# First tile's picks in two halves, its first expert rows gathered from the first half on

## The reference

```python
def ada_mod(c, w, b):
    return jnp.einsum('bd,de->be', jax.nn.silu(c), w) + b

def peer_ffn(h, w_q, sub_keys, peer_u, peer_v):       # for each block of 128 tokens xb
    q = jnp.einsum('td,de->te', xb, w_q).reshape(128, 8, 2, 128)
    s = jnp.einsum('thpk,pnk->thpn', q, sub_keys)
    s_top, i_top = lax.top_k(s, 16)                    # halves
    cand = s_top[:, :, 0, :, None] + s_top[:, :, 1, None, :]        # pairs, 256 a head
    cand_idx = i_top[:, :, 0, :, None] * 128 + i_top[:, :, 1, None, :]
    g_top, pos = lax.top_k(cand, 16)
    expert = jnp.take_along_axis(cand_idx, pos, axis=-1)
    g = jax.nn.softmax(g_top, axis=-1)
    u = jnp.take(peer_u, expert, axis=0)               # rows of 1024 floats
    act = gelu(jnp.einsum('thkd,td->thk', u, xb))
    vv = jnp.take(peer_v, expert, axis=0)
    return jnp.einsum('thk,thkd->td', g * act, vv)
```

## Time and profile before

| | us |
|---|---|
| median of 3 runs | 3175.43 (3171.84 to 3180.79) |
| the profiled execution | 3183.8 |
| its span | 3182.1 |
| PE, DVE, ACT, POOL busy | 2100.9, 1744.4, 853.1, 1008.9 |
| DMA | 860.04 MB, mean 270 GB/s |
| granted clock of TensorE, mean | 0.815 |

### The profile page before, as it was taken

One profiled execution on the slowest core, in us unless ns is written; L12 is line 12 of the kernel. 1 busy time (PEld: TensorE's weight loads), 2 busy tenths in 40 slices (PEclk: granted clock), 3 DMA queues, 4 the chain that ended last, 5 costly groups with the idle time before them and its releaser, 6 DMA issues.

```text
span 3182.1 us, 33988 instructions
## 1 busy us (share of the span) xinstructions
PE 2100.9 (66%) x11694; PEld 1433.0 (45%) x11694; DVE 1744.4 (55%) x3244; ACT 853.1 (27%) x1313; POOL 1008.9 (32%) x1064
## 2 busy tenths in 40 slices
PE   7889700344635755548620155899799989989998
PEld 4638200011222211222100011798689979977997
DVE  2365788623594258670658600565656656655664
ACT  3433200001021100220000000445544454464544
POOL 1000166666466566355666666000000000000000
PEclk9999955676867876669755567899899989999999
DMA  7664899999999999979999999455235545542553
GB/s 273 207 244 154 323 378 370 344 345 362 409 370 363 398 354 406 352 293 405 375 382 361 352 363 353 141 185 174 86 114 186 186 133 185 186 143 72 174 185 128
DMA packets 237519, 860.04 MB, mean 270 GB/s; under 512 B 27326, under 2 KB 27812, under 8 KB 237148
## 3 DMA queue, kind: packets, MB, share of 16 engines
q0 software_dynamic: 147456, 536.94, 44.5%
q1 hardware_dynamic: 87840, 318.81, 29.5%
q10 hardware_dynamic: 2108, 2.86, 0.3%
HBM read 857.43 MB, written 1.05 MB: 270 GB/s over the span
## 4 chain that ended last, share of the span: by engine, by line
PE 39%; DVE 18%; issue 12%; DMA 9%; another core or an unknown queue 5%; POOL 3%; ACT 2%; DVEq 1%; PEldq 1%; ACTq 0%; PEld 0%; POOLq 0%; SPq 0%
PE ps L1436 16%; DVE sb_arena L2486 13%; PE ps L1447 7%; DMA sb_arena<-in_peer_v,sb_arena 5%; PE ps L838 4%; POOL sb_arena L750 3%; PE ps L1193 3%; PE ps L1226 2%; PE ps L951 1%; DMA sb_w<-in_sb_w_q 1%; PE ps L1005 1%; DMA sb_w<-in_ada_w 1%; DVE sb_w_lo L644 1%; PE ps L1354 1%
## 5 line engine op out<-in xcount | busy, mean ns | idle before, releaser
L2486 DVE CUSTOM_DVE_ANT_0 sb_arena<-sb_arena,ps 128x1024 f32<-128x1024 f32 x512 | 601.8, 1218 | 93.9 <-issue 68.0
L644 DVE TENSOR_TENSOR sb_w_lo<-sb_w,sb_w_hi 128x1024 fp32r<-128x1024 f32 (+2 forms) x393 | 470.7, 1212 | 328.6 <-ACT sb_w_hi L630 325.6
L750 POOL DMA_INDIRECT sb_arena<-in_peer_u,sb_arena x512 | 484.4, 946 | 415.2 <-issue 166.6
L750 POOL DMA_INDIRECT sb_arena<-in_peer_v,sb_arena x512 | 494.1, 965 | 329.8 <-issue 137.1
L1193 PE MATMUL ps<-sb_arena 128*32 128x512 f32 x2048 | 369.8, 860 | 298.4 <-DMA sb_arena<-in_peer_v,sb_arena 258.9
L630 ACT ACTIVATE sb_w_hi<-sb_w 128x1024 fp32r<-128x1024 f32 (+2 forms) x398 | 407.4, 1040 | 289.3 <-DMA sb_w<-in_ffn 195.2
L1436 PE MATMUL ps<-sb_xT_hi,sb_w_hi 128*128 128x256 f32 x1408 | 400.1, 284 | 2.8 <-DVE sb_w_lo L644 2.8
L1436 PE MATMUL ps<-sb_xT_lo,sb_w_hi 128*128 128x256 f32 x1408 | 399.9, 284 | 0.0
L1436 PE MATMUL ps<-sb_xT_hi,sb_w_lo 128*128 128x256 f32 x1408 | 399.9, 284 | 0.0
L1193 PEld LDWEIGHTS ps<-sb_arena 128*32 128x32 f32 x2048 | 78.2, 135 | 571.6 <-issue 571.4
L644 POOL TENSOR_TENSOR sb_w_lo<-sb_w,sb_w_hi 128x1024 fp32r<-128x1024 f32 x5 | 12.0, 2397 | 909.1 <-ACT sb_w_hi L630 909.1
(11 more groups left out here) (434 smaller groups left out, 3005.0 us busy)
## 6 DMA issues: line engine op xcount, KB each, us to landing
sb_w<-in_ffn SPq DMA_DIRECT2D x264, 512.0 KB
sb_w<-in_ada_w SPq DMA_DIRECT2D x112, 512.0 KB
sb_w<-in_peer_w_q SPq DMA_DIRECT2D x48, 512.0 KB
sb_w<-in_kv_w SPq DMA_DIRECT2D x32, 512.0 KB
sb_w<-in_fox_w_in SPq DMA_DIRECT2D x24, 512.0 KB
sb_w<-in_ma_w_vo SPq DMA_DIRECT2D x16, 512.0 KB
sb_arena<-in_peer_u,sb_arena POOLq DMA_INDIRECT x512
sb_arena<-in_peer_v,sb_arena POOLq DMA_INDIRECT x512
```

The source lines that it names most:

```text
L644: e.tensor_tensor(lo, w, hi.bitcast(F32), ALU.subtract).then_inc(lo_ready, 1)
L750: pool.indirect_dma_start(ROW[:, r % ROWS, :], None, d[("peer_v" if kind else "peer_u") + str(layer)], bass.IndirectOffsetOnAxis(ap=(LISTE ...
L2486: v.tensor_tensor_reduce(out=x, in0=x, in1=PS[:, 0:2, :].rearrange("p a b -> p (a b)"), scale=1.0, scalar=0.0, op0=ALU.mult, op1=ALU.add, ...
```

## The change

`PICK_FIRST` becomes a list of two pickings of four heads each. Their buffers leave the arena's first 12,288 columns, where the ring `ROW` lies, for `XTF` and `WHF`. VectorE does `best_halves`, `best_pairs` and `chosen` for the first four heads and then for the last four; as `WHF` holds the upper part of the sub-keys' weights, it waits for the last sub-key product (`unit_used`) ahead of all of it. `picked`, `top_shifted` and `top_exp` now count 2 in this stage. GpSimd no longer enters `weave` by `stage_done`; it waits for the first `picked` ahead of row 0 and for the second ahead of row 64. ScalarE does four chunks of modulation, the first half's exponential, the other six chunks, and the second half's exponential.

```diff
-                c = dict(top_shifted=1, top_exp=1, picked=1)
+                c = dict(top_shifted=2, top_exp=2, picked=2)
...
-        PICK_FIRST = picking(0, SCORE, part(0, PH, PTOP * PTOP), part(4096, PH, PTOP, PTOP), A[:, 10240:12288])
+        PICK_FIRST = [picking(0, SCORE, XTF[:, 2048 + 1024 * n:3072 + 1024 * n].rearrange("p (b c) -> p b c", c=PTOP * PTOP),
+                              WHF[:, 1024 * n:1024 * n + 1024].rearrange("p (h a b) -> p h a b", a=PTOP, b=PTOP),
+                              WHF[:, 2048 + 1024 * n:3072 + 1024 * n], n * PH // 2, PH // 2) for n in range(2)]
...
-                    if kind == 0 and w and n in ((0,) if w == 2 else (0, PSLOTS // 2)):
-
-                        claim("picked", at(st, "picked", {2: 1, 4: 2, 6: 4}[w] + (n > 0)))
+                    if w == 0 and n == 0:
+                        claim("picked", at(st, "picked") - 1)
+                    elif kind == 0 and n in ((0,) if w == 2 else (0, PSLOTS // 2)):
+
+                        claim("picked", at(st, "picked", {0: -1, 2: 1, 4: 2, 6: 4}[w] + (n > 0)))
...
             for st in STAGES:
-                enter(pool, st)
+                if st["kind"] != "weave":
+                    enter(pool, st)
...
                 if st["ada"]:
                     f(GATE0, mod(5), ACT.Copy)
                     act.drain()
-                    modulations(st, 0, 6)
-                act.wait_ge(SEM["top_shifted"], at(st, "top_shifted", 1))
-                best = PICK_FIRST["best"]
-                f(best, best, ACT.Exp).then_inc(SEM["top_exp"], 1)
-                if st["ada"]:
-                    modulations(st, 6)
+                ends = (0, 4, len(st["ada"]))
+                for n in range(2):
+                    modulations(st, ends[n], ends[n + 1])
+                    act.wait_ge(SEM["top_shifted"], at(st, "top_shifted", n + 1))
+                    best = PICK_FIRST[n]["best"]
+                    f(best, best, ACT.Exp).then_inc(SEM["top_exp"], 1)
...
                 dve.wait_ge(SEM["score_out0"], at(st, "score_out0"))
-                best_halves(PICK_FIRST)
                 dve.wait_ge(unit_used, used(STAGES[st["n"] - 1]["unit0"]))
-                best_pairs(PICK_FIRST)
-                chosen(st, PICK_FIRST, 0)
+                for n, b in enumerate(PICK_FIRST):
+                    best_halves(b)
+                    best_pairs(b)
+                    chosen(st, b, n)
```

## The result

| | before | after |
|---|---|---|
| median of 7 runs each, same chip | 3177.11 (3171.84 to 3180.79) | 3192.10 (3184.70 to 3194.75) |
| ratio | | 1.0045, 95% interval 1.0028 to 1.0062 |
| the profiled execution, its span | 3183.8, 3182.1 | 3194.75, 3192.8 |
| granted clock of TensorE, mean | 0.815 | 0.810 |

By the ratio the change costs 14.3 us, with an interval of 8.9 to 19.7. The forecast was +8 us. Averaged as two independent measurements they give some 12.6 us, with 8.7 to 16.4 as the interval. The direction is as forecast, the size is above it, and the median of 3192.1 stands at the range's upper end of 3192.

The account below looks back on a forecast made before the run. The flow of bytes through DMA, not the picks, was taken to bound the kernel. Row 12's bytes, at 411.9 to 412.9 against 404.3, gave +8 us on the median 3175.4: 3183.4 us (+0.25%), range 3168 to 3192.

Parts of the forecast that it names:

- When the picks start: `topk` on VectorE: first MAX8 waits for the sub-key products, moving from 326.99 to some 331.5, +4.5 us.
- What two halves cost: Picks on VectorE: one half takes 29.6 us, two 59.2 against 54.5 us whole; first half picked at 361.1.
- What the early gathers do to the loads: End of `topk`: 12 early gathers share DMA evenly with weights, delaying the last `ada` unit 15.4 us, first dot product 16.6.
- Rival (b): During `ada` loads: they give way less to early gathers, +1 to +2 us, in the extreme -6.6 us; together chance 0.15.
- The hole: Before row 12 of the first window: little DMA between 403 and 412 us, some 9 us long.
- It is paid in full: From the first window to the end: the hole's whole length delays every later row and the chain on them.
- Rival (c): First window: 12 rows of stock improve its pace from 1.437 to 1.28 us a row, -10 us, 3165; chance 0.10.
- Rival (d): Early issue fails because a half waits for its exponential behind the weights; result slides to +3; no separate chance.
- The sum: Whole kernel: +8 us, from row 12 moving bytes 7.6 to 8.6 us late against 404.3; 3183.4 us on the median.
- ramp of 1.4 us: First gathers in the kernel before: 6 us at 313 instead of 410 GB/s, which the changed kernel was credited with avoiding.
- rival (a): Hole and boundary: restart from cold costs another 1.4 us, later boundary counts one to one; +10 to +14 us, chance 0.33.
- The rule of the Trainium skill: Row 12's gather: 2.0 us plus bytes over 436 GB/s, landing 3.2 us after issue, at 414.2; sum would be +6.6 us.

Follow-up runs that it names:

- e6: Changed kernel, but ScalarE takes the second half's exponential behind chunk 8 instead of behind all ten; ratio 1.0032 to the kernel before, price 10.2 us.
- e1: Changed kernel with the picks in halves, but GpSimd waits at the stage boundary again, so no row is gathered early; ratio 1.0025, price 7.6 us.
- e8: Changed kernel, loading only half of each `ada` unit in `topk` and multiplying with that half twice; ratio 1.0012 to the kernel before, +3.8 us.
- e12: Changed kernel with four rows early, `H` copied into PSUM ahead of the small loads, two modulation chunks moved to the norm stage; ratio 1.0026, +8.3 us.
- e5: Changed kernel measured once more, unaltered, in another series; ratio 1.0034 (1.0017 to 1.0051) to the kernel before, price 10.8 us.
- e9: Kernel before, with GpSimd clearing ten rows of its ring ahead of row 0, so the first gathers go out later; ratio 1.0034, price 10.8 us.
- e2: Changed kernel, but only four rows gathered early, GpSimd waiting for the stage boundary ahead of row 4; ratio 1.0001, price 0.3 us.
- e10: Changed kernel, but only eight rows gathered early, GpSimd waiting for the stage boundary ahead of row 8; ratio 1.0014, price 4.5 us.
- e3: Changed kernel, but ScalarE copies `H` into PSUM ahead of its small loads; ratio 1.0012 to the kernel before, price 3.6 us.
- e4: Kernel before, with ScalarE copying `H` into PSUM ahead of its small loads; ratio 1.0004, +1.2 us.

## Why the prediction came out as it did

**When the picks start: right.** Said: +4.5 us, right behind the last sub-key product. The first MAX8 is at +0.06.

**What two halves cost: the first right, the second not.** Said: 29.6 us each. The first takes 30.1; in it the exponential is ready at 364.20, 0.6 us ahead of the sum that needs it (one of 0.8 was said). The second takes 34.0 us to its last CAST, 4.7 more than the first up to the same place, with gaps of VectorE's own in it, so that 3.4 of the 9.8 us of slack behind the weights were left. e6 shows no price of this here; e1, e8 and e12 show the picks as the last to end where the weights do not hold the stage.

**What the early gathers do to the loads: right, with 3 us of play in it.** Said: 12 gathers, 1.25 us apart, sharing the flow evenly with the weights, last `ada` product at 396.8 (+65.2), boundary at 401.7 (+70.1), first dot product at 409.6 (+78.0). Measured: even shares, 1.25 us, +63.8, +68.3, +76.3. All came 1.4 to 1.8 us sooner than said. In the repeat e5 they are at +64.8, +71.4 and +79.3: the product 0.4 us sooner, the other two 1.3 us later than said. Rival (b), that the loads give way less, has 1.5 us of truth at most.

**The hole: right in place, and in length for the first trace.** Said: from 403 to 412 us, +71.4 to +80.4. The engines stop at 407.1 (+71.6) and move bytes again at 415.9 (+80.3). Row 12 was issued at +78.3 (said +79.4). In the repeat they stop at +71.8 and start at +83.3, with row 12 issued at +81.3.

**"It is paid in full": right as far as the runs can tell.** e9 shows it with the hole alone, and e2, e10 and e3 by shortening it. e4 adds little, as said above. One support of it was weaker than it read: the piece of 112 us in the chain is called "another core or an unknown queue" there, so the profile does not say that it is the gathers' queue. Rival (c), a better pace behind a stock of 12 rows, is there only for a short time. The flow missing up to 100 us behind the score copy is 2.6 us before and 11.4 after, up to 140 us 7.8 and 14.4: the kernel before has a dip at 430 to 440 us (277 GB/s) that the changed one has not at that place, and so 2.2 of 8.8 us come back. Up to 240 us it is 16.1 and 24.5, and they are lost again. VectorE's "issue" pauses in the window fell from 27.6 to 18.1 us (23.0 in the repeat), without a better pace of the window as a whole. Rival (d) did not occur.

**The sum: too small.** "I take 8" is the time from 404.3, where the kernel before has moved the same bytes, to the first bytes of row 12. Two terms of it were short.

The first is the restart. The sum gives the kernel after credit for the ramp of 1.4 us that its first gathers no longer have, and takes the flow to be whole again from the first bytes of row 12. But the ramp comes back behind the hole: in stretches of 1 us, what is missing against 410 GB/s behind 415.9 is 1.9 us in the kernel after, 1.9 in e5 and 1.7 in e9. This was in rival (a), with 1.4 us, but not in the forecast.

The second is the end of the stage. The sum moves ScalarE's last copy by the 15.4 us of the gathers and no more. In the first trace that was even 1.8 us too much, in the repeat 1.3 too little, because the last `ada` products ran at the lower clock there (e5, above). This is the other half of rival (a), a boundary that comes later; no run held the clock fixed, but in the trace ScalarE's last copy waits for just these matmuls.

With both, and row 12 taken from its first bytes (+80.3 and +83.3, where the sum has +80.7), the sum is 8 - 0.4 + 1.9 = 9.5 us in the first trace and 8 + 2.6 + 1.9 = 12.5 us in the repeat. The flow missing up to 100 us behind the score copy is 8.8 and 11.4 us, and the two ratios average to 12.6 us. That the forecast of 8 agrees with the 8.4 us of missing flow up to 240 us in the first trace is in part luck: there the stage ended 1.8 us sooner than said, which makes up for the restart. Behind the boundary two small steps were longer than said: row 12 is issued 2.0 us behind the first dot product (said 1.4) and moves bytes 2.0 us later (said 0.9 to 1.9).

What stays open is which hole most executions have, as only one of each kernel was profiled, and the rest of the first measurement: 14.3 us by the ratio, with 8.9 as its lower end, beside a trace with the shorter hole. I put the price at 9 to 16 us, and name no cause for what may be above 12.5.

The reading of the measurement followed: 0.25% was forecast with "within 0.3%" as the likeliest, at 0.34 to 0.45% it is slower. Had the restart been in the sum, 8 + 1.9 = 9.9 us would have been above the border of 9.5, and the chances for "slower" would have had to be above those for "same".

**The rule of the Trainium skill** that stood beside the sum, page "DMA: Bandwidth & Descriptors", section "Anatomy of one DMA" (about 2.0 us plus bytes over 436 GB/s, 3.2 us for a gather), can be held against e9: its first gather is issued at 399.30 into idle engines, and the dot product that waits for it starts at 404.07, 4.8 us behind. The trace does not agree with the 3.2 us. By that rule the sum would have been +6.6 us, which is further off than the one that was used.

## What to carry to other kernels

Where the flow of bytes sets the time, judge a reordering by one question: does it open a stretch without flow, and for how long? In these runs, work fetched early was worth nothing where it only changed places with other bytes in a full queue, and it cost the stretch in which its full ring then stood idle; so an early fetch should take as many entries as leave the ring enough to bridge the next fixed delay (here 4 of 12, for 8 us between the boundary and the first user). Where such a hole hangs on the end of a stage, ask what else moves that end: here TensorE's clock in its last products was worth 2 us. And before bytes are moved to an idle stage, see what stands behind their consumers in the engines' order there.

## What the hardware showed that was not expected

- A gather flow that restarts from empty engines takes some 8 to 10 us to come back to 410 GB/s: 303 and 323 GB/s from 416 to 424 us behind the hole of the kernel after, 220 and 324 from 400 to 410 behind that of e9, where the first rows come 2.0 us apart (404.07, 406.08) although one is issued in 1.25 us. On balance it is 1.7 to 1.9 us of missing flow.
- In the second half of the picks VectorE shows pauses of its own that the first half does not have: 3.32 us ahead of the CAST at 380.05. From its first MAX8 to the end of its last CAST the second half takes 29.1 us in e1, e2 and e12 (no row or four rows gathered early), 31.3 in e10 (eight), and with twelve 34.0 in the kernel after, 34.8 in e6, 34.1 in e8 and 37.0 in e5, but 29.1 in e3. So the pauses come with many early gathers, and not always; why was not tried.
- TensorE's products of the last `ada` units wait for weights, and their clock differs between executions of one kernel: 1.00 in the kernel after and 0.50 in e5 from 395 to 400 us, 1.05 against 1.92 us for the four matmuls of a unit.
- The same kernel before took 3040 us in one series and 3185 in the others, and the flow differs with it: e4, whose ratio to before is 1, has 405 GB/s from 12 to 240 us behind the last score copy, the profile before 381. Why the gathers run faster there is open; the record gives both the series of e4 and that of e5 the same chip number.
